# Norm statistics on a few columns: the heads' factors inside the exponential, the norms' factors spread by matmul

## The reference, cut to what matters

```python
def rmsnorm(x, g):
    xf = x.astype(jnp.float32)
    y = xf * lax.rsqrt(jnp.mean(xf * xf, axis=-1, keepdims=True) + NORM_EPS)
    return (y * g.astype(jnp.float32)).astype(x.dtype)
...
def qk_heads(t, g):
    bn, tn, _ = t.shape
    return rmsnorm_2(t.reshape(bn, tn, 2, B_HEADS_2, B_QK_DIM), g)
...
def diff_attention(q, k, v, lam):
    s = jnp.einsum('bqahd,bkahd->bahqk', q, k).astype(jnp.float32) * (B_QK_DIM ** -0.5)
    p = jax.nn.softmax(s, axis=-1)
    a = (p[:, 0] - lam * p[:, 1]).astype(v.dtype)
    return jnp.einsum('bhqk,bkhe->bqhe', a, v)
...
        q_lat = apply_rope(qk_heads(z_lat[..., B_Q:B_K], q_norm_g[l]), cos, sin)
        k_lat = apply_rope(qk_heads(z_lat[..., B_K:B_V], k_norm_g[l]), cos, sin)
...
        attn_lat = blocked_diff_attention(q_lat, k_all, v_all, lam)
```

## Time and profile before

| | |
|---|---|
| median of 3 runs | 3927.58 us (3925.65 to 3928.03) |
| profiled execution | 3924.05 us, its span 3922.2 us |
| mean granted clock of TensorE | 0.956 of full speed |
| busy: TensorE, its weight loads | 3605.9 us, 2877.1 us |
| busy: VectorE, ScalarE, GpSimd | 1608.5, 968.2, 2022.7 us |

### The profile page before, as it was taken

The page is one execution under the profiler, slowest core; times in us unless marked ns, Lnnn a source line. Parts: engine busy times, 40 slices in busy tenths (PEclk is TensorE's granted clock), DMA queues, the critical chain, the costliest instruction groups (busy, mean ns, idle before and its releaser), DMA issues.

```text
span 3922.2 us, 46006 instructions
## 1 busy us (share of the span) xinstructions
PE 3605.9 (92%) x18218; PEld 2877.1 (73%) x18218; DVE 1608.5 (41%) x2741; ACT 968.2 (25%) x2040; POOL 2022.7 (52%) x1216
## 2 busy tenths in 40 slices
PE   7898779898899999899998899999999998999999
PEld 5776557676678988768776686887668766777887
DVE  6744432333863321564355313431372554214430
ACT  2134333322201211221244312220121343112210
POOL 4454225564457898745333264665544332455655
PEclk9999879999899999999999999999999999999999
DMA  6623113332564443332111122322322111222322
GB/s 227 230 93 104 46 38 99 113 107 70 197 203 132 138 141 127 115 118 76 65 53 45 54 91 75 97 91 82 117 70 76 54 54 44 74 88 80 97 84 100
DMA packets 109863, 389.18 MB, mean 99 GB/s; under 512 B 12057, under 2 KB 16537, under 8 KB 108242
## 3 DMA queue, kind: packets, MB, share of 16 engines
q1 hardware_dynamic: 89280, 315.10, 24.7%
q10 hardware_dynamic: 20370, 71.13, 5.3%
HBM read 379.86 MB, written 6.32 MB: 98 GB/s over the span
## 4 chain that ended last, share of the span: by engine, by line
PE 67%; DVE 8%; ACT 2%; issue 1%; POOL 1%; DMA 0%; DVEq 0%; ACTq 0%; SPq 0%
PE ps L305 19%; PE ps L307 18%; PE ps L306 18%; PE ps L1320 3%; PE ps L1332 1%; PE ps L395 1%; PE ps L900 1%; PE ps L396 1%; PE ps L397 1%; DVE ada L1784 1%; DVE junk L1784 1%; DVE small_d L1377 1%; PE ps L1300 1%; DVE ps L942 1%; PE ps L567 1%
## 5 line engine op out<-in xcount | busy, mean ns | idle before, releaser
L2329 POOL CAST whi<-raw 128x1024 fp32r<-128x1024 f32 (+1 forms) x606 | 618.1, 1020 | 1838.3 <-DMA raw<-in_w 1838.2
L2331 POOL TENSOR_TENSOR wlo<-raw,whi 128x1024 fp32r<-128x1024 f32 (+1 forms) x606 | 1416.9, 2338 | 48.5
L305 PE MATMUL ps<-hhi,whi 128*128 128x512 f32 x2056 | 853.5, 415 | 126.3 <-DVE hlo L951 23.7
L306 PE MATMUL ps<-hlo,whi 128*128 128x512 f32 x2056 | 828.1, 403 | 0.0
L307 PE MATMUL ps<-hhi,wlo 128*128 128x512 f32 x2056 | 827.3, 402 | 0.0
L305 PEld LDWEIGHTS ps<-hhi,whi 128*128 128x128 f32 x2056 | 395.4, 192 | 257.3 <-issue 45.9
L307 PEld LDWEIGHTS ps<-hhi,wlo 128*128 128x128 f32 x2056 | 395.7, 192 | 96.7
L306 PEld LDWEIGHTS ps<-hlo,whi 128*128 128x128 f32 x2056 | 396.7, 193 | 94.7 <-issue 6.7
L305 PE MATMUL ps<-chi,whi 128*128 128x256 f32 x864 | 259.3, 300 | 9.7 <-DVE mc_lo L867 3.9
L306 PE MATMUL ps<-clo,whi 128*128 128x256 f32 x864 | 248.6, 288 | 0.0
L307 PE MATMUL ps<-chi,wlo 128*128 128x256 f32 x864 | 247.9, 287 | 0.0
(11 more groups left out here) (368 smaller groups left out, 6398.1 us busy)
## 6 DMA issues: line engine op xcount, KB each, us to landing
raw<-in_w SPq DMA_DIRECT2D x574, 512.0 KB, 3.5
ada<-in_ada ACTq DMA_DIRECT2D x96, 512.0 KB, 3.9
raw<-in_w SPq DMA_DIRECT2D x16, 384.0 KB, 3.2
att_toe<-toe_dram ACTq DMA_DIRECT2D x12, 256.0 KB, 3.3
raw<-in_w SPq DMA_DIRECT2D x16, 192.0 KB, 2.3
x<-in_x SPq DMA_DIRECT2D x4, 512.0 KB, 9.8
cond<-in_cc ACTq DMA_DIRECT2D x2, 1024.0 KB, 4.9
kc_dram<-kc ACTq DMA_DIRECT2D x2, 1024.0 KB, 3.9
```

The lines of the kernel that those rows point to most:

```text
L305: nc.tensor.matmul(o, whi[:, buf, c], hi[:, k, 0:n], start=(k == 0), stop=False)
L306: nc.tensor.matmul(o, whi[:, buf, c], lo[:, k, 0:n], start=False, stop=False)
L2329: nc.gpsimd.tensor_copy(whi[:, buf, 0:c], raw[:, buf, 0:c]).then_inc(slab_hi, 1)
L2331: nc.gpsimd.tensor_tensor(wlo[:, buf, 0:c], raw[:, buf, 0:c], whi[:, buf, 0:c].bitcast(F32), ALU.subtract).then_inc(slab_split, 1)
```

## The change

**Norms.** The square tile becomes the stationary operand, one 128-token block after the other, and a column of 1/1024 the moving one: each block gives one column of 128 means with tokens on the partitions. A 512-token norm has 4 columns of statistics, a 256-token one 2, the group norm 16. Root and reciprocal work on these columns. Then TensorE, which now waits for the reciprocal in its own order, turns them into what the apply steps read: per block the factor column, broadcast to 128 columns, is the stationary operand and the identity the moving one (4 matmuls; 2 for 256 tokens; 16 for the group norm).

**Queries (latents in both layers, context).** A new epilogue, `FactorHeads`. Statistics by block as above with two moving columns (one for each half of the partitions), into one bank for all eight tiles, 64 (32) columns. One root behind the last tile, one reciprocal, a multiplication by 1/8, and one by -1 for the second set of columns. The queries are left without their factor; the factor is the exponential's scale and, negated, the multiplier of the maximum, each a column of a tile in place of a number in the instruction.

**Context keys (both layers).** Statistics of tile m go to rows 2m and 2m+1 of 16 rows (a slice of the new constant `HALVES` is the stationary operand and the squares the moving one), with one root and one reciprocal on 16 x 256 behind the last tile. From ten steps behind a tile's first, in steps of their own, two matmuls spread a tile's two rows over 64 partitions each, and VectorE multiplies. The gain is now the scale of ScalarE's copy.

**Latent keys** keep `QKHeads`; their first statistics wait for the queries' last rotation.

**Order.** In the softmax stage keys and queries of the context alternate from the keys' ninth step on; in layer 1 the context's keys come ahead of its values and alternate with them. Some parts of the context wait for the last key as well as for the last query.

```diff
 EPS_COL, EPS_SMALL, ONE_COL, R1024, R256, MINUS_COL = range(3 * P, 3 * P + 6)
-N_CST = 3 * P + 6
+HALVES = 3 * P + 6
...
+                if m == 0:
+                    for c in self.before:
+                        pe.wait_ge(*c())
...
+        class FactorHeads(Epilogue):
...
+                self.lag = 10 if over else 2
...
+            def ready(self, m):
+                return (self.qo, self.qo0 + m + 1) if self.over else (self.rr, self.rr0 + 3)
+            def rooted(self):
+                return self.rt, self.rt0 + 1
...
+            def tensor(self, pe, i):
...
+                if self.has(m):
+                    if self.rope is None:
+                        pe.wait_ge(*freed(self.g.tile[m]))
+                    else:
+                        pe.wait_ge(self.cp, self.cp0 + 2 * m + 2)
+                        if self.qs0 + 2 * m >= 4:
+                            pe.wait_ge(self.qs, self.qs0 + 2 * m - 2)
+                        nc.tensor.matmul(self.mixes[m % 2], self.swaps, self.raws[m % 2], start=True, stop=True)
+                    if m == 0:
+                        for c in self.before:
+                            pe.wait_ge(*c())
+                    if self.over:
+                        mm = nc.tensor.matmul(self.compact, cst[:, HALVES + 14 - 2 * m:HALVES + 30 - 2 * m], self.sq[m % 2],
+                                              start=(m == 0), stop=(m == self.tiles - 1))
+                    for j in range(0 if self.over else self.per):
+                        c = 2 * (self.per * m + j)
+                        mm = nc.tensor.matmul(self.compact[:, c:c + 2], self.sq[m % 2][:, j * P:(j + 1) * P],
+                                              blocks64[:, 0:P:HD], start=(m == 0 and j == 0), stop=True,
+                                              skip_group_check=True)
+                    mm.then_inc(self.mm, 1)
+                m = i - self.lag
+                if self.over and self.has(m):
+                    pe.wait_ge(self.rr, self.rr0 + 1)
+                    if m >= len(self.over):
+                        pe.wait_ge(self.qo, self.qo0 + m - len(self.over) + 1)
+                    o = self.over[m % len(self.over)]
+                    for a in range(2):
+                        mm = nc.tensor.matmul(o[HD * a:HD * a + HD, :],
+                                              ident[0:16, 2 * m + a:2 * m + a + 1].to_broadcast([16, HD]), self.factor,
+                                              start=True, stop=True)
+                    mm.then_inc(self.sp, 1)
...
+            def scalar(self, act, i):
+                if i - 2 == self.tiles - 1:
+                    act.wait_ge(self.mm, self.mm0 + self.tiles)
+                    rows = self.compact.shape[0]
+                    nc.scalar.activation(self.factor[:, 0:self.cols], self.compact, ACT.Sqrt,
+                                         bias=cst[0:rows, EPS_COL:EPS_COL + 1]).then_inc(self.rt, 1)
...
+                    if self.rope is None:
+                        nc.scalar.activation(self.kept(m), self.out(m), ACT.Copy, scale=self.gain)
+                        nc.scalar.activation(self.sq[m % 2], self.out(m), ACT.Square).then_inc(self.free(m), 1)
+                    else:
...
+                    nc.vector.tensor_tensor(mix, mix, self.rope[:, 1, :], ALU.mult).then_inc(self.qs, 1)
...
+                if m == self.tiles - 1:
+                    f = self.factor[:, 0:self.cols]
+                    dve.wait_ge(self.rt, self.rt0 + 1)
+                    nc.vector.reciprocal(f, f).then_inc(self.rr, 1)
+                    if not self.over:
+                        dve.wait_ge(self.rr, self.rr0 + 1)
+                        nc.vector.tensor_scalar(f, f, SCALE, None, ALU.mult).then_inc(self.rr, 1)
+                        dve.wait_ge(self.rr, self.rr0 + 2)
+                        nc.vector.tensor_scalar(self.factor[:, self.cols:2 * self.cols], f, -1.0, None, ALU.mult)\
+                            .then_inc(self.rr, 1)
+                m = i - self.lag
+                if self.over and self.has(m):
+                    d = self.dst(m)
+                    dve.wait_ge(self.sp, self.sp0 + m + 1)
+                    if self.rope is not None:
+                        dve.wait_ge(self.qs, self.qs0 + 2 * m + 2)
+                    nc.vector.tensor_tensor(d, self.over[m % len(self.over)], d, ALU.mult).then_inc(self.qo, 1)
...
+                if k == self.K:
+                    pe.wait_ge(self.rr, self.rr0 + 1)
+                    for g, o in enumerate(self.stats):
+                        for j, b in enumerate(blocks):
+                            c = len(blocks) * g + j
+                            mm = nc.tensor.matmul(o[:, b], self.factor[:, c:c + 1].to_broadcast([P, P]), ident,
+                                                  start=(j == 0), stop=True, skip_group_check=True)
+                    mm.then_inc(self.sp, 1)
                 if k >= self.K:
...
+                for j, b in enumerate(blocks):
+                    c = len(blocks) * g + j
+                    mm = nc.tensor.matmul(self.stats[0][:, c:c + 1], self.sq[k % 2][:, b], cst[:, self.mean:self.mean + 1],
+                                          start=(k == 0 and j == 0), stop=(k == self.K - 1 or self.group[k + 1] != g),
+                                          skip_group_check=True)
+                mm.then_inc(self.sum, 1)
 
             def scalar(self, act, i):
...
-                    for s in self.stats:
-                        a = nc.scalar.activation(s, s, ACT.Sqrt, bias=cst[:, EPS_COL:EPS_COL + 1])
-                    a.then_inc(self.rt, 1)
+                    c = len(self.stats) * self.n // P
+                    nc.scalar.activation(self.factor[:, 0:c], self.stats[0][:, 0:c], ACT.Sqrt,
+                                         bias=cst[:, EPS_COL:EPS_COL + 1]).then_inc(self.rt, 1)
...
             def vector(self, dve, i):
                 K = self.K
                 if i == K:
+                    f = self.factor[:, 0:len(self.stats) * self.n // P]
                     dve.wait_ge(self.rt, self.rt0 + 1)
-                    for s in self.stats:
-                        v = nc.vector.reciprocal(s, s)
-                    v.then_inc(self.rr, 1)
-                    dve.wait_ge(self.rr, self.rr0 + 1)
+                    nc.vector.reciprocal(f, f).then_inc(self.rr, 1)
+                    dve.wait_ge(self.sp, self.sp0 + 1)
                 k = i - K - 1
                 if 0 <= k < K:
...
+            def q_factor(self, t, a, negated=False):
+                h, b = self.units[t]
+                c = 2 * (self.per * h + b + 8 * self.per * negated) + a
+                return self.factor[:, c:c + 1]
 
...
-                                                 scale=SCALE, bias=self.neg_at[t % 2][:, a:a + 1],
+                                                 scale=self.q_factor(t, a), bias=self.neg_at[t % 2][:, a:a + 1],
...
-                        nc.vector.tensor_scalar(small[1][:, a:a + 1], small[0][:, a:a + 1], -SCALE,
+                        nc.vector.tensor_scalar(small[1][:, a:a + 1], small[0][:, a:a + 1],
+                                                self.q_factor(t, a, True),
...
-                        QKHeads(con, lambda m: kc[:, m, :], col(("k_g", l)), banks67, [cC[:, :], cD[:, :]], clear=clear),
+                        FactorHeads("k", con, lambda m: kc[:, m, :], col(("k_g", l)), ps[0:16, 7 * 512:7 * 512 + TC],
+                                    [cC[:, :], cD[:, :]], kc_factor[:, :], [pb(6, TC)], clear=clear),
...
         query_c = Gemm("q0", 8, KT, chi, clo, TC,
-                       QKHeads(con, lambda m: qc[:, m, :], col(("q_g", 0)), banks67, [cC[:, :], cD[:, :]]))
+                       FactorHeads("q", con, lambda m: qc[:, m, :], col(("q_g", 0)), pb(7, 32), [cC[:, :], cD[:, :]],
+                               qc_factor[:, :], before=[key_c.epi.rooted]))
...
-            L["k"] = Gemm(f"k{l}", 8, KT, hhi, hlo, T, heads_of(1, lambda m: k2[:, m, 0:T], "k_g"))
+            rope_clear = [lambda l=l: (rope_loaded, 16 * (l + 1)), lambda l=l: (swap_scaled, 2 * (l + 1))] + prior
+            L["q"] = Gemm(f"q{l}", 8, KT, hhi, hlo, T, FactorHeads(
+                "q", lat, lambda m: q2[:, m, :], col(("q_g", l)), pb(7, 64), sqs, q_factor[:, :], (), rope, swapg[:, 0, :],
+                [pb(4, T), pb(5, T)], raws, rope_clear), ready=L["norm1"].ready, clear=[lambda: key_c1.epi.ready(7)])
+            L["k"] = Gemm(f"k{l}", 8, KT, hhi, hlo, T, QKHeads(
+                lat, lambda m: k2[:, m, 0:T], col(("k_g", l)), [pb(2, T), pb(3, T)], sqs, rope, swapg[:, 1, :],
+                [pb(4, T), pb(5, T)], raws, rope_clear + [L["q"].epi.turned], [L["q"].epi.turned]))
...
+        def alternate(keys, n, others):
+            mixed = [(keys, i) for i in range(n)]
+            for j, other in enumerate(others):
+                mixed += ([(keys, n + j)] if n + j < keys.steps else []) + [other]
```

(6 more changed lines are left out.)

97 lines of the change are left out of this document (77 added, 20 removed).

## The result

| | before | changed |
|---|---|---|
| median, 11 runs each | 3927.8 us | 3936.0 us |
| profiled execution, span | 3922.2 us | 3935.0 us |
| mean granted clock of TensorE | 0.956 | 0.949 |

The ratio is 1.002, 95% interval 1.001 to 1.0029: 0.2% slower, at the very edge of what can be told from no change, where the forecast was 0.5% faster (3909, 3888 to 3933). The change also moves the activations by 480 bytes, and that by itself changes the time; what this means for the +8 is told with e1 and e5.

A forecast was written before the change was run, and what follows sets the result against it. TensorE, busy 92% of the span, was taken to bound the kernel, so only its idle stretches could pay. Savings of 30.4 against costs of 2.6, 5.8 and 3.0 gave -19.0: median 3909 us, range 3888 to 3933.

The forecast's parts named there:

- the sum of the norms: All norms together, from bare norms to group, MLP, cross and memory norms: -24 us before the added statistics work.
- The spread: Matmuls turning factor columns into 128x512 on TensorE: 0.11 us a pass, 1.19 a bare norm, 3.6 the group norm.
- Saved 2.30, four times: -9.2: Four bare norms (input, norm 2 of both layers, norm 1 of layer 1): 4.03 us removed, 1.73 added each.
- I take 751.7 ... -9.0: Group norm: the GEMM behind it resumes at 751.7 instead of 760.66, saving 9.0 us (6.2 to 9.4).
- The MLP norm: MLP norm with the context's norm 2: chain of 5.90 us falls to 2.75, saving 3.1 (2 to 4).
- The cross norm's 2.6: Cross-attention and memory norms: shorter reciprocals save 2.6 us (1 to 3.5), 2.1 of it at the cross norm.
- Statistics on TensorE: 88 groups in norms and query tiles: eight narrow passes at 0.11, 0.88 us a group; +2.6 us in all.
- Pointers: Attention's exponential and maximum: +0.09 and +0.06 us an instruction; +5.8 (0 to 19) latent, +3 (0 to 4.8) context.
- Nothing counted at the first query tile: Start of latent attention's heads: latent key tiles and steps behind the queries taken as hidden or unchanged, no cost.
- closing stage: Layer 1's context keys with final norm and norm 1: -4.5 us (0 to -9), including some 4 waiting for a spread.
- The gains of the woven stages don't come, and the pointers cost on every unit: Rival: in-order spread waits cancel the context parts' gains, pointers cost +10 us; 3925 us, no difference; 13%.
- Narrow passes cost 0.155: Rival for every norm and query tile: narrow passes take 0.155 us each, +33 instead of +2.6; 3939 us; 9%.

The follow-up runs named there:

- e1: Kernel before with only the new norm class and its small tiles; old heads, attention and order: 3892.8 us, ratio 0.9914.
- e5: Kernel before with 96 bytes left free ahead of the activations' zone, nothing else: 3882.0 us, ratio 0.9883.
- e7: e1 with 384 bytes more, so its activations begin where the changed kernel's do: 3923.5 us, ratio 0.9990.
- e2: Changed kernel with the old norm class; new heads, pointers in attention and order stay: 3926.3 us, ratio 1.0004.
- e3: Changed kernel with immediate numbers again in both attentions' exponential and maximum, the queries' factor left out: 3920.4 us, ratio 0.9984.
- e14: Kernel before with new norms only where they paid, layer 1's context keys by rows, alternating order, early rotation table, activations at start 128: 3876.7 us, ratio 0.9873.
- e17: e14 with layer 1's context keys stored in four parts as finished, values at the end: 3871.1 us, ratio 0.9856.

## Why the prediction was wrong, point by point

**The step that failed first is the sum of the norms, and in it the price of their new TensorE work.** "The spread" took 0.11 a pass from a stream at the full clock, 1.19 for a bare norm and 3.6 for the group norm. Over the changed kernel's norms the distance of two spread passes is 0.19 in the mean; 53 of 87 are above 0.2, not counting the first of each spread, and the two spreads measured 1.65 and 5.2. The half-speed level meets the change's own work: it stays through the input norm's narrow groups to 35.1 us, it sets in during the group norm's statistics, where the kernel before is at 1.00, and at norm 2, where the clock falls in both kernels (2409.7 before, 2421.0 now), it now falls in the middle of the spread. Term by term: "Saved 2.30, four times: -9.2" came out as 1.4 to 2.2 in three norms (e7) and as a loss of 2.1 to 3.1 in the input norm. "I take 751.7 ... -9.0" for the group norm came out as 5.1 when the GEMM resumes and some 3 at the end of the stage: 2.7 by the clock in the statistics, 1.6 in the spread, and the rest because I forgot what GpSimd would do beside VectorE. The MLP norm gave 1.7 (1.5 in e7) for 3.1 (whose new chain adds up to 2.70, not 2.75): of the -4.3 in the table 2.7 lie ahead of the norm, in a half-speed stretch near 900 us that moves from kernel to kernel, also in those with the old norms (e5). The cross norm's 2.6 can't be told: the stretch has -1.6, but e2, with the old norm, has -1.3 there. Norms alone: -24 forecast before the statistics' term, and +10.8 measured at equal start (e1 against e5). The stretches named here don't add up to that; e7's 178 to 322 us, with the context's norm 1 that I hadn't priced, is +3.3, but the unchanged kernel at other starts ranges from -1.9 to +2.4 there.

**Statistics on TensorE: right at the full clock.** A group in a query tile takes 0.81 to the next GEMM instruction (1715.69 to 1716.50), and the tile's period is 7.36 where it was 7.31, both from the starts of their first passes; forecast were 0.88 and no growth. The 0.155 of the earlier trace rows was start-up, as taken. What the term lacked is the lower clock, where a load and its narrow matmul take 0.21; 135 of the 639 distances between one-column passes are that long, 63 of them in the input norm.
The Trainium skill, "TensorE: Matmul & The Clock Gate", section "LDWEIGHTS (loading the stationary operand)", has a load take P / 1.2 ns, with P the columns of the stationary operand and not its rows; for the 128 x 128 loads here that is 107 ns whatever the matmul's width. (The prediction's "128 rows" should read 128 columns.) The medians of 112 ns between one- and two-column passes agree. The 25 ns that its section "Back-to-back issue gap" gives 1 to 64 columns appear here only between the first two passes of a group (0.03, 46 times in the changed kernel), never from load to load.

**Pointers: the duration right, the price too low.** +0.09 and +0.06 an instruction are measured to the digit. The term of 5.8 + 3 = 8.8 should have been 15.6 (e3), since beside the lengthened chain the granted clock is lower: 0.73 for 0.78 in the context's attention, 0.85 for 0.95 in the second half of latent attention (e3). My upper bound of 19 + 4.8 held it.
The Trainium skill, "ScalarE: Activation LUTs", section "What ACT_TABLE_LOAD costs", says 93 ns for each pointer operand; 91 and 89 agree.

**Nothing counted at the first query tile: wrong.** I counted the change's two new waits there and not the transfer that was already within 1.0 us of the path. It took 8.0, part by the wait (4.05), part by the clock behind it. Where the closing stage became shorter (e2: -9.7, e14: -7.9), this tile took most of it back (7.8, 6.1), since the stores begin only behind the last key. e17 bears this out: with the stores spread out the wait falls from 3.2 to 1.4 and the tile takes back some 1.5 in place of 6.1.

**The closing stage: right for the heads, gone with the norms.** e2 has -9.7 (forecast -4.5, to -9), e7 +3.8, and both together -0.2, not -5.9. TensorE's wait for the final norm's factor, the "some 4" of the forecast, is there:

```profile
1602.68 0.17 DVE L1084 RECIPROCAL norm_f<-norm_f 128x4 f32<-128x4 f32 x1
...
1602.90 2.08 PE L1040 MATMUL ps<-cst,norm_f 128*128 128x128 f32 x8 [3.44 <-DVE norm_f L1084]
...
1604.99 0.41 PE L309 MATMUL ps<-clo,whi 128*128 128x256 f32 x1
```

3.44 idle, eight spread matmuls at 0.21 each and the context's passes behind at half speed. Why the two halves lose 5.7 against their sum in this stage isn't settled by a run. The same is so from 417 to 628 us, where e2 has +4.7, e7 -1.5 and both together +8.8.

**The rivals.** "The gains of the woven stages don't come, and the pointers cost on every unit" (13%, 3925) named a wait and a price that both occur and was 11 us short, for want of the clock and the transfer. "Narrow passes cost 0.155" (3939) reached the right time by luck: no narrow pass settles there, they take 0.112 at the full clock and 0.213 at half. (By its own terms a group at 0.15 a pass costs 0.34 more, not 0.31.)

## What to carry to other kernels

Price a short operation on TensorE twice, at the clock of its own stretch, and ask whether the new work keeps that clock: here the same norm saved 1.4 to 2.2 us in three places and lost 2 to 3 at the start, where its narrow matmuls ran at half speed throughout. Before shortening a stage, look at what is within a microsecond of the path at its end, transfers above all; the time won there goes to them first. And when two builds differ in pace where their programs are alike, compare addresses before the edits, and give the kernel before the same start as the changed one: 96 bytes of padding were worth more than any edit of the schedule tried here.
